# A two-layer model with a third block on one core: the opening's transfers and the order of its first operations

## The reference, cut to what matters

```
c_act = jax.nn.silu(c)
for i in range(DEPTH):
    mod = c_act @ mod_w[i] + mod_b[i]
    sh1, sc1, g1, sh2, sc2, g2, sh3, sc3, g3 = jnp.split(mod, 9, axis=-1)
    h = modulate(rmsnorm(x, norm_g[i, 0]), sh1, sc1)      # h * (1 + scale) + shift
    x = x + FFN_RES * g1[:, None, :] * swiglu(h, ffn_w13[i, 0], ffn_w2[i, 0])
    ...
```

## Time and profile before

| | us |
|---|---|
| median of 3 runs | 1733.41 (1732.05 to 1733.92) |
| profiled execution, its time | 1733.04 |
| profiled execution, its span | 1730.9 |
| TensorE busy | 1655.9 (96%) |
| VectorE busy | 1284.3 (74%) |
| ScalarE busy | 930.3 (54%) |

### The profile page before, as it was taken

How to read it: one execution, slowest core, us unless ns; L and a number is a source line. 1 busy time by engine, 2 the same in 40 slices (tenths; PEclk the granted TensorE clock), 3 DMA queues, 4 the chain that set the end, 5 groups by cost and what they waited for, 6 DMA issues and landing times.

```text
span 1730.9 us, 31804 instructions
## 1 busy us (share of the span) xinstructions
PE 1655.9 (96%) x11246; PEld 1494.3 (86%) x11246; DVE 1284.3 (74%) x2125; ACT 930.3 (54%) x1673; POOL 94.5 (5%) x164
## 2 busy tenths in 40 slices
PE   6899999999999999999999999999999999999998
PEld 5799989988899889998877888889998789988886
DVE  6888888668888888886656666668999666456665
ACT  1544457644444454445466655564549875555553
POOL 2000010300000100001000000010001000000000
PEclk9999999999999999999999999999999999999999
DMA  9888867857888878876535566645464346445651
GB/s 349 303 298 300 299 184 193 170 193 261 297 301 297 269 261 296 294 260 179 183 108 158 178 193 197 185 128 192 147 181 137 109 155 196 134 152 190 193 183 61
DMA packets 129433, 361.94 MB, mean 209 GB/s; under 512 B 10059, under 2 KB 58715, under 8 KB 119489
## 3 DMA queue, kind: packets, MB, share of 16 engines
q1 hardware_dynamic: 111200, 262.18, 47.1%
q10 hardware_dynamic: 12432, 78.65, 14.0%
q0 software_dynamic: 5712, 19.92, 3.5%
HBM read 353.47 MB, written 7.23 MB: 208 GB/s over the span
## 4 chain that ended last, share of the span: by engine, by line
PE 66%; DVE 17%; issue 7%; ACT 6%; DMA 2%; POOL 1%; ACTq 1%; DVEq 0%; POOLq 0%
PE ps L883 45%; PE ps L1224 9%; PE ps L1225 4%; DVE w_lo L232 4%; DVE arena L387 3%; DVE arena L2877 2%; ACT w_hi L226 2%; ACT w_hi L1282 1%; DVE resid L1501 1%; DVE w_lo L1293 1%; PE ps L467 1%; PE ps L744 1%; DMA arena<-in_small 1%; DVE act_s L1370 1%; DMA gate_scratch<-gcol 1%
## 5 line engine op out<-in xcount | busy, mean ns | idle before, releaser
L883 PE MATMUL ps<-t_both,w_hi 128*128 128x256 f32 x3852 | 709.5, 286 | 9.1 <-DVE arena L2851 4.4
L883 PEld LDWEIGHTS ps<-t_both,w_hi 128*128 128x128 f32 x3852 | 600.1, 191 | 21.5 <-issue 9.4
L883 PE MATMUL ps<-t_both,w_lo 128*128 128x256 f32 x1926 | 545.0, 283 | 0.0
L1293 DVE TENSOR_TENSOR w_lo<-raw,w_hi 128x1024 fp32r<-128x1024 f32 x258 | 313.7, 1222 | 82.5 <-ACT w_hi L1282 82.4
L883 PEld LDWEIGHTS ps<-t_both,w_lo 128*128 128x128 f32 x1926 | 367.6, 191 | 0.2
L232 DVE TENSOR_TENSOR w_lo<-raw,w_hi 128x1024 fp32r<-128x1024 f32 x240 | 288.3, 1223 | 106.3 <-ACT w_hi L226 106.0
L1282 ACT ACTIVATE w_hi<-raw 128x1024 fp32r<-128x1024 f32 x258 | 268.9, 1053 | 119.0 <-PE ps L883 79.1
L226 ACT ACTIVATE w_hi<-raw 128x1024 fp32r<-128x1024 f32 x240 | 247.2, 1052 | 136.5 <-PE ps L883 97.1
L1224 PE MATMUL ps<-t_both,w_hi 128*128 128x512 f32 x640 | 226.7, 398 | 0.0
L883 PE MATMUL ps<-w_hi,g_hi 128*128 128x512 f32 x440 | 177.3, 403 | 14.1 <-DVE g_lo L1373 11.9
L1225 PE MATMUL ps<-t_both,w_lo 128*128 128x256 f32 x640 | 179.7, 281 | 0.0
(11 more groups left out here) (396 smaller groups left out, 1757.3 us busy)
## 6 DMA issues: line engine op xcount, KB each, us to landing
raw<-in_stream SPq DMA_DIRECT2D x498, 512.0 KB, 4.5
arena<-in_mod_w ACTq DMA_DIRECT2D x72, 1024.0 KB, 7.2
grow<-gate_scratch POOLq DMA_DIRECT2D x6, 512.0 KB, 7.8
u_scratch<-u_keep ACTq DMA_DIRECT2D x1, 3072.0 KB, 36.8
arena_for_products<-mem_scratch POOLq DMA_DIRECT2D x3, 1024.0 KB, 7.1
mem_scratch<-arena_for_products POOLq DMA_DIRECT2D x1, 2048.0 KB, 13.0
arena<-u_scratch POOLq DMA_DIRECT2D x8, 256.0 KB, 3.8
small<-in_small POOLq DMA_DIRECT2D x1, 1368.0 KB, 11.1
```

Source lines behind the costliest of these rows:

```text
L883: last = TE.matmul(out, lhs, rhs, start=start and i == 0, stop=stop and i == 2)
L1293: VE.tensor_tensor(w_lo[:, s, :], raw[:, s, :], w_hi[:, s, :].bitcast(F32), ALU.subtract).then_inc(lo_done, 1)
```

## The change

c gets a transfer of its own on ACT's queue and a semaphore of its own; cols is fetched from column 8 on. SP waits for the first half chunk, then asks for x (before: POOL), then for blocks 0 and 1. Small is asked for behind the second half of chunk four instead of chunk two's, and in POOL's program it stands behind the row statistics. On VectorE three chunks come first, then the scalings, then low parts 0 and 1, then chunk four and low part 2. High parts 0 and 1 stand behind the squares on ACT. On TensorE turn 0 stands ahead of the bias products, the wait for rows and positions behind them, eight fillers' calls are gone, and the other six wait for the fifth product of chunk four (`mod_step` at 29).

```diff
+        c_in = sem("c_landed")
...
         def _(sp):
+            sp.wait_ge(mod_landed[0][0], 16)
+            sp.dma_start(x[:, :, :], a["x"].rearrange("(q p) d -> p q d", p=P)).then_inc(x_in.sem, x_in.up(16))
             for s in range(RING):
                 if s == 2:
                     sp.wait_ge(mod_landed[0][1], 32)
...
-            for dst, src in ((cols[:, :], a["cols"]), (cst[:, :], a["const"])):
+            for dst, src in ((cols[:, 8:], a["cols"][:, 8:]), (cst[:, :], a["const"])):
...
-            pool.dma_start(x[:, :, :], a["x"].rearrange("(q p) d -> p q d", p=P)).then_inc(x_in.sem, x_in.up(16))
...
-            pool.wait_ge(mod_landed[1][1], 16)
-            pool.dma_start(small[:, :], a["small"]).then_inc(small_in.sem, small_in.up(16))
...
         def _(act):
+            act.dma_start(cols[:, 0:8], a["cols"][:, 0:8]).then_inc(c_in, 16)
             for c in range(3):
                 for half in range(2):
                     mod_load(act, half, c)
-            act.wait_ge(first_in.sem, first_in.n)
+            act.wait_ge(c_in, 16)
             E.activation(cact[:, :], col("c", 0, 8), ACT.Silu).then_inc(A.sem, A.up())
...
                 if scale_after:
-                    dve.wait_ge(first_in.sem, first_in.n)
                     dve.wait_ge(A.sem, silu_at)
                     for c in range(scale_after):
                         mod_products(dve, c, range(KT), first=True)
-                    for h in range(blocks["hi"]):
-                        split_lo(dve, h)
...
         def _(act):
-            for h in range(2):
-                split_hi(act, h)
             for half in range(2):
                 mod_load(act, half, 3)
-        blocks["hi"] = 2
-        normalize(lambda q: x[:, q, :], lambda q: ar(XN, QT, D)[:, q, :], first_norm, landed_first=x_in, scale_after=2)
+        normalize(lambda q: x[:, q, :], lambda q: ar(XN, QT, D)[:, q, :], first_norm, landed_first=x_in, scale_after=3)
         blocks["hi"] = 3
 
         @block.scalar
         def _(act):
-            split_hi(act, 2)
+            for h in range(3):
+                split_hi(act, h)
 
         @block.vector
         def _(dve):
-            for c in range(2, PRE):
+            dve.wait_ge(first_in.sem, first_in.n)
+            for h in range(2):
+                split_lo(dve, h)
+            for c in range(3, PRE):
                 mod_products(dve, c, range(KT), first=True)
             split_lo(dve, 2)
-        bias_at = bias_products()
+
+        @block.gpsimd
+        def _(pool):
+            pool.wait_ge(mod_landed[0][1], 32)
+            pool.dma_start(small[:, :], a["small"]).then_inc(small_in.sem, small_in.up(16))
 
         @block.tensor
         def _(pe):
             pe.wait_ge(first_in.sem, first_in.n)
+            mod_turn(pe, 0, first=True)
+        bias_at = bias_products()
+
+        @block.tensor
+        def _(pe):
             pe.wait_ge(inputs.sem, inputs.n)
-            mod_turn(pe, 0, first=True)
             mod_turn(pe, 1, first=True)
-            keep_busy(ps[4], 8)
             mod_turn(pe, 2, first=True)
+            pe.wait_ge(mod_step, 3 * 8 + 5)
             keep_busy(ps[4], 6)
             mod_turn(pe, 3, first=True)
```

More of the change, by code:

```diff
@@ L535, in _ @@
         def _(act):
-            split_hi(act, 2)
+            for h in range(3):
+                split_hi(act, h)
         @block.vector
         def _(dve):
-            for c in range(2, PRE):
+            dve.wait_ge(first_in.sem, first_in.n)
+            for h in range(2):
+                split_lo(dve, h)
+            for c in range(3, PRE):
                 mod_products(dve, c, range(KT), first=True)
             split_lo(dve, 2)
+        @block.gpsimd
[4 more added lines that the diff above has]
+        def _(pe):
+            pe.wait_ge(first_in.sem, first_in.n)
+            mod_turn(pe, 0, first=True)
         bias_at = bias_products()
@@ L546, in _ @@
         def _(pe):
-            pe.wait_ge(first_in.sem, first_in.n)
             pe.wait_ge(inputs.sem, inputs.n)
-            mod_turn(pe, 0, first=True)
             mod_turn(pe, 1, first=True)
-            keep_busy(ps[4], 8)
             mod_turn(pe, 2, first=True)
+            pe.wait_ge(mod_step, 3 * 8 + 5)
             keep_busy(ps[4], 6)
```

## The result

| | before | after |
|---|---|---|
| median, us | 1732.35 (12 runs, 1730.47 to 1733.92) | 1736.14 (12 runs, 1734.19 to 1737.20) |
| ratio | | 1.0021, 95% interval 1.0013 to 1.0028 |
| profiled execution, its time | 1733.04 | 1737.01 |
| profiled execution, its span | 1730.9 | 1735.1 |

A forecast was written before the change was run, and what follows sets the result against it. Bound: TensorE's opening chain to the columns' add, VectorE's nearly equal with 0.6 us of room. Span 1730.9 - 1.2 = 1729.7, plus 2.1 is 1731.8; against a median 0.4 higher, 1732.2 us; range 1729.2 to 1735.6.

The forecast's parts named there:

- Rival B: Opening: TensorE's chain alone decides, 43.28 becomes 37.9, a gain of 5.3 us to 1728.1; chance 0.05.
- The landing: Second half of chunk three arrives at 26.7 us: 9.62 MB through, 0.9 in the first 5 us, then 402 GB/s.
- the forecast gain of 1.2 us: Opening up to the columns' add: turn 3 ends at 42.1 us against 43.28, passed on one to one.
- The limit of about 358 GB/s: HBM limit for one core: landing near 29.5, a loss of some 1.6 us; counted only as a hint.
- turns in order of arrival: TensorE's opening: turn 0 before the bias products, turns 1 and 2 to 35.3 us, then idle, turn 3 ending at 42.1.
- rival C: TensorE's array stays at its lower clock into the first FFN, 1734.5 or, in a long form, 1740.2; chance 0.17.
- short form: Lower clock for three microseconds of the first FFN's products: together a loss of 2.3 us, net 1.1 slower, 1734.5.
- The 12 fillers still stand right before turn 3: TensorE's opening: the reason given against the array staying at its lower clock; no size of its own.
- weight loads of 333 ns after the add: TensorE behind the columns' add: a sign named in advance that the forecast would be wrong.
- The 16 fillers (3.57 us) are gone: TensorE's opening: filler products removed between turns, their 3.57 us taken off the chain.
- the 2.0 us taken as its lower bound: Load of c on ACT's queue: bounded from below by the fastest landing of any, a 256 KB store on SP.

The follow-up runs named there:

- e5: Changed kernel with the eight filler calls put back ahead of turn 0, where TensorE idles; the hole stays: 1732.10 us, ratio 0.9998.
- e3: Changed kernel with the transfer of small asked for behind chunk two's second half again, ahead of the row statistics: 1739.42 us, ratio 1.0036.
- e2: Kernel before without the eight filler calls between turns 1 and 2, the other six waiting for chunk four's fifth product: 1736.81 us, ratio 1.0022.
- e1: Changed kernel with eight filler calls (16 instructions) put back between turn 2 and the wait for chunk four's fifth product: 1730.01 us, ratio 0.9989.
- e4: Kernel before with only c by its own transfer, and silu waiting for it: 1732.32 us, ratio 0.9997.
- e6: Changed kernel with the hole filled by 2 calls of 512 columns (4 instructions) behind turn 2: 1732.05 us, ratio 0.9994.
- e7: Changed kernel, old TensorE program length, scalings back between chunks two and three, low parts 1 and 2 behind chunk four: 1729.72 us, ratio 0.9982.
- e9: Kernel before with the same filler time in wider calls, TensorE's program 18 instructions shorter, no hole: 1734.64 us, ratio 1.0012.
- e8: Changed kernel, scalings before chunk three, low parts behind chunk four, blocks 0 and 1 after chunk three's landing, 6 plus 8 filler calls: 1730.61 us.

## Why the prediction was wrong, point by point

**Right.** The changed opening ran as the prediction described it. VectorE's first product started at 6.64 us (predicted near 6.5), and it waited for half chunks 1.8, 2.3, 1.0, 0.7 and 0.6 us afterwards (5 or more predicted). Chunk four came without a gap behind the late landing, TensorE was idle from 35.1 to 38.7 us, and the bias weights cost nothing. Rival B, TensorE's chain of the earlier trace rows shortened by 5.3 us, was rightly put aside.

**A term mis-sized.** The landing was put at 26.7 us and measured at 28.1. The two stretches up to it, to be read with the earlier trace rows:

```profile
0.00:5.00 5.00, 0.00 (x0) 0.00 (x0) 0.00 (x0) 0.25 (x1) 3.92 (x11) 1.00 0.55 161
5.00:28.10 23.10, 13.19 (x55) 11.47 (x56) 14.62 (x20) 5.59 (x12) 5.15 (x10) 1.00 1.01 396
```

In the first 5 us 0.81 MB went and not 0.9, with no second queue to begin with; the pace was 396 and not 402 GB/s; and 0.81 + 23.1 x 0.396 = 9.95 MB had gone at the landing and not 9.62. That is 1.4 us, and with it the forecast gain of 1.2 us at the add was gone: 43.32 for 43.37. The limit of about 358 GB/s, which the prediction took from the Trainium skill (DMA: Bandwidth & Descriptors, Specifications) and set against the rows, was not borne out here either: 396 GB/s over 23.1 us.

**The step that failed first: turns in order of arrival, costed without the clock.** The prediction named the mechanism as rival C, gave it 0.17, and priced its short form at 2.3 us of loss. It was what happened: 2.2 us at the first hidden tile, and 1.7 to 2.3 over the four traces with a hole and a late clock. "The 12 fillers still stand right before turn 3" was the reason to doubt it, and the reason was wrong: with a hole ahead (3.7 us in the changed kernel, 3.6 in e5, 5.5 in e3, 1.5 and 1.7 in e2), the same 12 fillers left the array at its lower level; without the hole, with 12 or 16 narrow or 4 wide instructions in its place, it had risen by the transposes (before, e1, e4, e6, e7, e9). In e8, with no hole but 16 fillers only, it had not (182/225/370 ns). So a late rise doesn't need a hole. Filling the hole always added fillers too, and no run parts these two further. The prediction named the sign of this itself, weight loads of 333 ns after the add, and they are there.

**The step that failed most: "The 16 fillers (3.57 us) are gone."** Their time was taken off and the shorter program was taken to cost nothing. It cost 4.0 us at 332 us (e5 against the changed kernel, in the medians and in the traces). The traces in which TensorE ran 16 to 18 instructions fewer than before (the changed kernel, e2, e3, e9) all have the wait of 2.0 to 2.3 us there; those with 0 to 12 fewer (before, e1, e4 to e8) have none. In e3 no low clock follows the wait, and VectorE's instructions lose 2.6 us there against before, where they lose 4.0 in the changed kernel: so the wait is some 2.6 us of the step of 4.0, the low clock 1.4. No case of the prediction held this. Without it the loss is gone, but the forecast doesn't stand: e5, the changed kernel with the old length, has no gain at the add to speak of (43.12 for 43.37), a trace 0.4 us longer than before (1731.3 for 1730.9), and a ratio (0.9998, 0.9989 to 1.0007) that can't tell the forecast gain of 1.2 us from none. That its median is 1732.10, where 1732.2 was predicted, is luck: the prediction counted from 1733.41, the median of three runs, and over twelve runs before has 1732.35.

The Trainium skill (Runtime: NRT & Kernel Launch, Instruction fetch mechanics) says that an engine's instructions are fetched ahead in blocks of 16 KiB by a DMA queue of its own and that crossing from one to the next is mostly hidden. The trace agrees in the size (16 KB in queue 8) and differs in the hiding at this place: 2.3 us in the open.

**What stays open.** e9, with the filler time kept, shows that a shorter program is enough to bring the wait. That the block at 332 us is TensorE's own and late because ScalarE's transfer fills the DMA engines is inferred from the counts in the table above, which agree in all eleven traces; the profile doesn't say whose block it is, and no run took that transfer away. Where between 12 and 16 instructions the fetch moves was not tried. Of the 4.0 us, the stretch of low clock behind the wait is tied to it only by standing behind it in three of the four traces that have the wait at all; e3 has the wait and runs on at full clock.

## What to carry to other kernels

Before fillers, or any instructions, are taken out of an engine's program, ask two things that its own line of the timeline doesn't show: what clock the engine has when the critical work arrives, and where in the later program the fetches of code will fall. Compare the starts of the same instructions in both traces from end to end; a loss that comes in 290 us behind the edit can't be found in the part that was edited. And where transfers bound a stage, count the bytes that must be through before the last one needed (1.4 us off in the prediction, 0.2 in e8), and put work that needs none of them into the gaps and not behind the landing (e7).

## What the runs showed of the hardware

- TensorE was busy without a gap from 15.8 to 42.6 us in before, with weight loads of 333 ns in turns and fillers up to the end of it, the lower level; busy time in the profile doesn't say that the array is at its upper level. The rise differed from trace to trace of kernels with the same fillers: during the 28 fillers in e1 (38.7 us), 42.8 in before. In e1 it also fell again behind the sparse transposes (row below, PEclk 0.50) and that run was still faster than before.

```profile
45.60:49.00 3.40, 3.39 (x17) 3.38 (x17) 2.46 (x5) 3.19 (x5) 0.00 (x0) 0.50 1.02 417
```

- The column of the granted clock reads 1.00 up to the first rise (42.8 us in before, 51.4 in the changed kernel) whatever the durations say; from there it follows them.
- The 4 KB load of c, first on an empty queue, landed 1.8 us after its issue, less than the 2.0 us taken as its lower bound.
